# Sharing the expert sum of a PEER layer between VectorE and GpSimd, row by row

## The reference

```python
q = jnp.einsum('td,de->te', xb, wq).reshape(PEER_BLOCK, PEER_HEADS, 2, PEER_DH)
s = jnp.einsum('thpc,hpnc->thpn', q, subkeys).astype(jnp.float32)
...
g = jax.nn.softmax(top, axis=-1)
hid = jnp.einsum('thkd,td->thk', u_tab[idx], xb).astype(jnp.float32)
act = (g * jax.nn.gelu(hid)).astype(xb.dtype)
return jnp.einsum('thk,thkd->td', act, v_tab[idx])
```

## Time and profile before

| | |
|---|---|
| median of 3 runs | 4849.47 us (4844.11 to 4852.52) |
| the profiled execution | 4842.91 us, its span 4841.2 us |
| busy: PE / DVE / ACT / POOL | 68% / 65% / 21% / 28% of the span |
| DVE adds L1805 | 640, 817.9 us, 1278 ns each |
| DVE dots L1789 | 640, 779.9 us, 1219 ns each |
| POOL gathers L1600 | 640, 776.8 us, 1214 ns each; 2112.2 us idle before them |
| DMA moved | 1579.68 MB, mean 326 GB/s |
| peer rows of tiles 0 to 4 | from about 640 us to 3680 us; the tail is what follows |

### The profile page before, as it was taken

How to read it: one execution, slowest core, us unless ns; L and a number is a source line. 1 busy time by engine, 2 the same in 40 slices (tenths; PEclk the granted TensorE clock), 3 DMA queues, 4 the chain that set the end, 5 groups by cost and what they waited for, 6 DMA issues and landing times. The chain is left out here.

```text
span 4841.2 us, 38032 instructions
## 1 busy us (share of the span) xinstructions
PE 3289.7 (68%) x10576; PEld 1748.2 (36%) x10576; DVE 3157.7 (65%) x6031; ACT 993.4 (21%) x2018; POOL 1372.4 (28%) x1287
## 2 busy tenths in 40 slices
PE   8679786455987687446455556985904777777776
PEld 6466542333544333334211112432401333333322
DVE  0121277896767688889766665887687666766754
ACT  1120111243211110235323231221101111111121
POOL 0000023322223234312111112332234454444432
PEclk9789898566998899567666667997957998989989
DMA  5343489777989899866799998998879999999988
GB/s 212 103 138 144 161 326 372 284 251 283 360 329 374 313 369 399 295 221 223 287 412 408 407 399 307 378 360 326 351 247 372 421 421 421 421 421 421 421 359 335
DMA packets 311757, 1579.68 MB, mean 326 GB/s; under 512 B 36536, under 2 KB 96108, under 8 KB 155823
## 3 DMA queue, kind: packets, MB, share of 16 engines
q0 software_dynamic: 158288, 1151.42, 60.1%
q1 hardware_dynamic: 122750, 377.41, 20.5%
q10 hardware_dynamic: 30560, 49.03, 2.7%
HBM read 1526.49 MB, written 50.99 MB: 326 GB/s over the span
## 5 line engine op out<-in xcount | busy, mean ns | idle before, releaser
L1600 POOL DMA_INDIRECT peer_row<-in_peer_uv,peer_staged x640 | 776.8, 1214 | 2112.2 <-DVE peer_y L1805 2013.4
L1789 DVE SCALAR_TENSOR_TENSOR peer_row<-peer_row,peer_x 128x1024 f32<-128x1024 f32 x640 | 779.9, 1219 | 183.4 <-DMA peer_row<-in_peer_uv,peer_staged 151.3
L1805 DVE SCALAR_TENSOR_TENSOR peer_y<-peer_row,peer_coef,peer_y 128x1024 f32<-128x1024 f32 x640 | 817.9, 1278 | 0.0
L1968 PE MATMUL tail_y<-peer_row,tail_diag 128*128 128x512 f32 x896 | 441.2, 650 | 308.5 <-ACT tail_diag L1981 308.5
L1968 PE MATMUL tail_y<-tail_row,tail_diag 128*128 128x512 f32 x896 | 432.8, 641 | 130.9 <-ACT tail_diag L1981 130.9
L245 PE MATMUL pr_b<-pr_xT,pr_w 128*128 128x256 f32 (+2 forms) x1152 | 389.8, 502 | 110.0 <-DMA pr_xT<-in_xT 79.2
L829 PE MATMUL gs_gp<-gs_xT,gs_w 128*128 128x256 f32 (+2 forms) x1152 | 393.5, 496 | 51.1 <-DMA gs_w<-in_w_gate 46.2
L1968 PEld LDWEIGHTS tail_y<-peer_row,tail_diag 128*128 128x128 f32 x896 | 181.7, 208 | 567.2 <-issue 384.8
L1927 POOL DMA_INDIRECT peer_row<-in_peer_uv,tail_staged x224 | 259.3, 1158 | 307.1 <-PE tail_y L1968 237.0
L1927 POOL DMA_INDIRECT tail_row<-in_peer_uv,tail_staged x224 | 253.3, 1131 | 281.0 <-PE tail_y L1968 245.0
L245 PEld LDWEIGHTS pr_b<-pr_xT,pr_w 128*128 128x128 f32 x1152 | 225.6, 197 | 272.7 <-issue 180.3
(11 more groups left out here) (216 smaller groups left out, 4350.9 us busy)
## 6 DMA issues: line engine op xcount, KB each, us to landing
sa_kc<-in_cache_k SPq DMA_DIRECT2D x128, 512.0 KB, 14.4
sa_vc<-in_cache_v SPq DMA_DIRECT2D x128, 512.0 KB, 12.9
pr_w<-in_w_in SPq DMA_DIRECT2D x27, 2048.0 KB, 10.9
gs_w<-in_w_gate SPq DMA_DIRECT2D x36, 1024.0 KB, 9.6
rt_w<-in_w_q SPq DMA_DIRECT2D x24, 1024.0 KB, 8.8
gs_w<-in_w_br SPq DMA_DIRECT2D x24, 512.0 KB, 5.0
gs_w<-in_w_br SPq DMA_DIRECT2D x12, 1024.0 KB, 7.8
mx_w<-in_w_out SPq DMA_DIRECT2D x6, 2048.0 KB, 12.3
```

The source lines that it names most:

```text
L1600: pool.indirect_dma_start(out=self.row[b][:], out_offset=None, in_=dr["peer_uv"], in_offset=bass.IndirectOffsetOnAxis(ap=self.staged[slot] ...
L1789: v.scalar_tensor_tensor(out=self.row[b][:, 0:D], in0=self.row[b][:, 0:D], scalar=1.0, in1=self.x1[:], op0=ALU.mult, op1=ALU.mult, accum_o ...
L1805: v.scalar_tensor_tensor(out=self.y[:], in0=self.row[b][:, D:2 * D], scalar=self.coef[:, col:col + 1], in1=self.y[:], op0=ALU.mult, op1=AL ...
L1968: done = pe.matmul(part[:], diag[r % (2 * ROWS)][:], row[place(j, k)][:, D + hf * 512:D + (hf + 1) * 512], start=j == 0 and k == 0, stop=j ...
```

## The change

In the front's tiles the rows with odd k (1 and 3 of each unit, 320 of 640) are no longer added by DVE. POOL does it, directly before the gather that reuses the buffer: a tensor_scalar scales the v half in place by its coefficient, a tensor_tensor adds it to a second accumulator. This is the tile `out`, which is free between the store of one tile and the norm of the next; the first such row of a tile writes it with the tensor_scalar alone. The norm first adds `out` to `y` on DVE. POOL's loops are unrolled in Python, since each wait now has a constant value. In the first gathers of the tail POOL also adds the two odd rows of tile 4's last unit.

```diff
         def fetch(pool, m, k, slot):
 
             b = slot % 2 * ROWS + k
-            pool.wait_ge(self.added, ROWS * m + ROWS + k + 1)
-            apart(pool, dr["unwaited"])
+            if m >= 2 and k % 2:
+                self.add_second(pool, m - 2, k)
+                pool.wait_ge(self.added_second, self.second_through(m - 2, k))
+            elif m >= 2:
+                pool.wait_ge(self.added, self.first_through(m - 2, k))
             pool.indirect_dma_start(
...
+    def add_second(self, pool, m, k):
+
+        n, j = divmod(m, UNITS)
+        b, col = j % 2 * ROWS + k, ROWS * j + k
+        v_row, coef = self.row[b][:, D:2 * D], self.coef[:, col:col + 1]
+        pool.wait_ge(self.weighted, m + 2)
+        if j == 0 and k == 1:
+            if n:
+                pool.wait_ge(self.y_stored, 16 * n)
+            pool.tensor_scalar(self.out[:], v_row, coef, None, ALU.mult).then_inc(self.added_second, 1)
+        else:
+            pool.tensor_scalar(v_row, v_row, coef, None, ALU.mult).then_inc(self.scaled_second, 1)
+            pool.wait_ge(self.scaled_second, self.second_through(m, k) - n - 1)
+            pool.wait_ge(self.added_second, self.second_through(m, k) - 1)
+            pool.tensor_tensor(self.out[:], self.out[:], v_row, op=ALU.add).then_inc(self.added_second, 1)
...
     def norm(self, v, n):
-        v.wait_ge(self.added, ROWS * UNITS * n + ROWS * (self.units_of(n) + 3))
-        if n >= self.tail:
+        if n < self.tail:
+            v.wait_ge(self.added, self.first_through(UNITS * n + UNITS - 1, ROWS - 2))
+            v.wait_ge(self.added_second, self.second_through(UNITS * n + UNITS - 1, ROWS - 1))
+            v.tensor_tensor(self.y[:], self.y[:], self.out[:], op=ALU.add).then_inc(self.joined, 1)
+            v.wait_ge(self.joined, n + 1)
...
-        if adding:
+        if adding and k % 2 == 0:
             self.add(v, pn, pj, k)
...
-                        pool.wait_ge(self.added, added_through(r - len(self.row)))
-                        apart(pool, dr["unwaited"])
+                        m, k = divmod(r - len(self.row), ROWS)
+                        if k % 2:
+                            self.add_second(pool, m, k)
+                            pool.wait_ge(self.added_second, self.second_through(m, k))
+                        else:
+                            pool.wait_ge(self.added, self.first_through(m, k))
...
-                if n == first and j == 0:
+                if n == first and j == 0 and k % 2 == 0:
                     self.add(v, n - 1, UNITS - 1, k)
```

More of the change, by code:

```diff
@@ L1561, in __init__ @@
         self.added = sem("added")
+        self.added_second = sem("added_second")
+        self.scaled_second = sem("scaled_second")
+        self.joined = sem("joined")
         self.gelued = sem("gelued")
@@ L1603, in fetch, with tile @@
             ).then_inc(self.row_loaded[b], 16)
-        def units(pool, n, i):
-            for s in range(self.BLOCK):
-                m = n * UNITS + i * self.BLOCK + s
-                pool.tensor_copy(self.staged[s][:], self.index[:, bass.ds((i * self.BLOCK + s) * ROWS, ROWS)])\
+        def tile(pool, n):
+            pool.wait_ge(self.picked, self.KSTEP * n + self.KSTEP)
+            pool.tensor_copy(self.index[:], self.index_next[:]).then_inc(self.indexed, 1)
+            pool.wait_ge(self.indexed, n + 1)
+            for j in range(UNITS):
+                if j == (LATE if n in self.late else 0):
+                    load_score(pool, n + 1)
+                m = n * UNITS + j
+                slot = j % self.BLOCK
+                pool.tensor_copy(self.staged[slot][:], self.index[:, ROWS * j:ROWS * (j + 1)])\
                     .then_inc(self.staging, 1)
@@ L1614, in units @@
                 for k in range(ROWS):
-                    fetch(pool, m, k, s)
-        def tile(pool, n, late=False):
-            blocks, half = UNITS // self.BLOCK, LATE // self.BLOCK
-            pool.wait_ge(self.picked, self.KSTEP * n + self.KSTEP)
-            apart(pool, dr["unwaited"])
-            pool.tensor_copy(self.index[:], self.index_next[:]).then_inc(self.indexed, 1)
-            pool.wait_ge(self.indexed, n + 1)
-            apart(pool, dr["unwaited"])
-            if not late:
-                load_score(pool, n + 1)
-            start = 0
-            if late:
-                with pool.Fori(start, half) as i:
-                    units(pool, n, i)
-                load_score(pool, n + 1)
-                start = half
-            with pool.Fori(start, blocks) as i:
-                units(pool, n, i)
+                    fetch(pool, m, k, slot)
         @block.gpsimd
@@ L1639, in _, with first_through, late_through, second_through @@
             load_score(pool, 0)
-            n = 0
-            for stop in sorted({0, *self.late}):
-                if stop - n > 1:
-                    with pool.Fori(n, stop) as i:
-                        tile(pool, i)
-                elif stop - n == 1:
-                    tile(pool, n)
-                tile(pool, stop, late=stop in self.late)
-                n = stop + 1
-            assert n == self.tail
+            for n in range(self.tail):
+                tile(pool, n)
+    def first_through(self, m, k):
+        return 3 * ROWS + m * (ROWS // 2) + k // 2 + 1
+    def late_through(self, r):
+        before = ROWS * UNITS * self.tail
+        return 3 * ROWS + before // 2 + r - before + 1
+    def second_through(self, m, k):
+        return m * (ROWS // 2) + k // 2 + 1
+    def add_second(self, pool, m, k):
[12 more added lines that the diff above has]
+            pool.tensor_tensor(self.out[:], self.out[:], v_row, op=ALU.add).then_inc(self.added_second, 1)
     def scalar_open(self, act, part):
@@ L1802, in add @@
             v.wait_ge(self.weighted, UNITS * n + j + 2)
-        v.wait_ge(self.added, ROWS * UNITS * n + ROWS * (j + 3) + k)
+        v.wait_ge(self.added, self.first_through(UNITS * n + j, k) - 1)
         col = ROWS * j + k
@@ L1905, in nth @@
             return per_tile * n + ROWS * j + k
-        def added_through(r):
-            return 3 * ROWS + r + 1
+        added_through = self.late_through
         @block.gpsimd
@@ L1979, in diagonals @@
                     r = nth(n, j, k)
-                    act.wait_ge(self.added, added_through(r - 2 * ROWS))
+                    if r - 2 * ROWS >= nth(first, 0, 0):
+                        act.wait_ge(self.added, added_through(r - 2 * ROWS))
                     act.activation(diag[r % (2 * ROWS)][:], ident[:], ACT.Copy,
```

3 lines of the change are left out of this document (2 added, 1 removed).

## The result

| | before | after |
|---|---|---|
| median of 4 runs each (same chip) | 4846.8 us | 5352.2 us |
| lowest to highest | 4842.4 to 4852.5 | 5344.1 to 5357.7 |
| ratio, 95% interval | | 1.104 (1.102 to 1.106) |
| profiled run, its span | 4842.9, 4841.2 us | 5344.1, 5342.3 us |

The change makes the kernel 10.4% slower. The forecast was 5220 us, 7.6%, in a range of 4980 to 5460.

The account below looks back on a forecast made before the run. Row transfers bound dense projections (DVE next), DVE the prompt stage, cache transfers the sample stage. Projections +125, middle stages +170, prompt and sample +43, tile ends +30, tail below 5: about +370 on 4842.9, forecast 5220 us, range 4980 to 5460.

Parts of the forecast that it names:

- POOL's price for a row, 2.9 us: On POOL, from its copies' slope: tensor_scalar about 1.0 us plus tensor_tensor about 1.9 us; upper bound 5.8 us a row.
- The third rival: POOL's arithmetic much slower than its copy, toward 5.8 us a row: unit 23.3 us, total 5700 us; chance 7%.
- The unit without collisions, 12.7 us: POOL's four-row unit unhindered: copy 0.19, three gaps of 0.89, gathers 3.76, 0.31 between gathers, row work 5.8 us.
- Unrolling: 0: Unrolling POOL's loops changes nothing, since the register instructions cost less than the gathers they stand between.
- Collisions, +4.8 us a unit: POOL held by DVE: four new instructions 0.8 us each, gathers 1.1, copy 0.24, late even-row adds 0.3; unit 17.5 us.
- DVE held, two thirds of POOL's work: POOL's reads hold DVE's dots and adds 3.9 us a unit, less 2.56 us of adds removed: +1.3 us net.
- Dense projections, +125 us: Projection stages, 32 units: from 13.6 us to POOL's 17.5 us, +3.9 us each.
- The middle stages, +170 us: All other stages of about 17 us, 85 units: +2.0 us each, between +0.5 and +3.9.
- Prompt and sample, +43 us: Prompt and sample stages, 43 units of 25.2 us: POOL has time, DVE's holding costs +1 us each.
- Ends of tiles, +30 us: Five tile ends: a DVE join of about 1.2 us and POOL's wait for the store of `out`, 6 us each.
- Tail, below 5 us: Tail from 3680 us: only two of four rows of one unit are touched, below 5 us.
- The first rival's gain, -144 us: The offload works, POOL neither holding DVE nor hardly held; unit about 13.9 us, total 4705 us; chance 6%.

Follow-up runs that it names:

- the writing kernels: The changed kernel with memsets to an unread tile instead of POOL's arithmetic, odd rows dropped: 5.2 us a row 5027.21 us, 2.4 us a row 4799.25 us.
- the kernels above: The changed kernel, 5352 us; it without POOL's arithmetic, odd rows and join, 4760 us; the latter with POOL memsets of 5.2 us a row, 5027 us.
- The long write: Changed kernel with eight memsets to an unread tile, 5.2 us a row, replacing POOL's scaling and adding; odd rows and join dropped: 5027.21 us, ratio 1.038.

## Why the prediction was right, and where its sizes were off

The sign and the mechanism were right: POOL's unit becomes the bound, and its reads hold DVE. The time, 5352 us, is 132 us above the forecast and inside its range. That it is no further off owes something to luck, since misses of opposite sign met. By the forecast's own steps:

- **POOL's price for a row, 2.9 us.** Mis-sized: 2.84 + 2.34 = 5.2 us. The tensor_scalar, taken at 1.0, is the larger miss; the copies' slope gave the copy and not the arithmetic. The third rival, arithmetic slower than a copy, was true at 90% of its 5.8 us. Its unit, 23.3 us, and its time, 5700 us, were not: it kept the forecast's gaps and collisions, which were both too large, and the dense unit is 19.1.
- **The unit without collisions, 12.7 us.** With the measured prices it is 0.19 + 0.27 + 3.76 + 0.30 + 2 x 0.27 + 2 x (2.86 + 2.34 + 0.08) = 15.6 us. The price's miss (+4.6) was partly met by the three gaps of 0.89 that are 0.27 in unrolled code (-1.9), which I had read as a wait and priced as one. "Unrolling: 0" was right in time (ratio 1.000).
- **Collisions, +4.8 us a unit.** 19.1 - 15.6 = 3.5 in the dense stretches: somewhat less. A POOL instruction is held by 0.08 us (tensor_scalar, 2937 against 2860) or 0.28 (tensor_tensor, 2619 against 2340) on average, much less than the 0.8 taken: 0.7 us a unit instead of 3.2. The gathers, at 1415 ns against 940 alone, give 1.9 instead of 1.1, the copy 0.3; POOL's waits for a late add would be the rest.
- **DVE held, two thirds of POOL's work.** Right in direction, and shown by the writing kernels; right in size too. Without the adds DVE is busy 2793.6 us, with POOL's reading 3330.4: 537 us more, of which 6 are the join, or 3.3 us a unit where 3.9 was taken. Net of the relief, DVE's busy time rose by 172.7 us, about +1.0 us a unit where +1.3 was taken. 326 of the 537 us are the dots and adds. 80 sit in the small instructions that make the coefficients: over 128x4 elements 272 of them took 451 ns on average, 156 before. Most of the rest is in the front's own instructions, as the scans into `at_sums` (93.0 us before, 130.6 now).
- **Dense projections, +125 us:** +134, by two misses that cancel. The dense unit lost 19.1 - 13.6 = 5.5 us and not 3.9. But only 22 of the 32 units had stood in the dense stretches; 22 x 5.5 = 121 us, and the ten others, around the stages' starts and gates, lost little.
- **The middle stages, +170 us:** +321, the term that failed. "On average already near 17.5" let me take half of the dense units' loss. With POOL's ideal unit at 15.6 and its real one at 19.1, these 85 units had no slack: with the 30 us of the tile ends taken out, 291 us, they lost 3.4 us each, near the upper end I had named (+3.9). By the stage table of the kernels above, the relief gave these stages 37 us, POOL's time took 163 and the reading, with the ends of tiles, 195.
- **Prompt and sample, +43 us:** +33. The slack was there: with 25 us a unit, POOL at 70% and 57% busy had room, and the long write cost these stages 2.8 us. The 33 are 67 us of reading less 37 us of relief.
- **Ends of tiles, +30 us:** the join waited 28.4 us in all for POOL's last addition and took 1.22 us itself; the wait of POOL for the store of `out`, which I had feared, was 0.6 us. About the right sum, by the other half of the term.

```profile
L1824 DVE TENSOR_TENSOR peer_y<-peer_y,peer_out 128x1024 f32<-128x1024 f32 x5 | 6.1, 1221 | 28.4 <-POOL peer_out L1662 28.4
```

- **Tail, below 5 us:** +10.9. The long write has +7.0 there, without reading; what makes it is open.
- **The first rival's gain, -144 us,** was more than the idea holds: adds that cost nothing give 82 us. The middle stages gave 37 us and not 128, the prompt and sample stages 37 and not 56. What else limits the middle stages' units was not separated.
- **The range.** Its terms give 5020 and 5430 us; the prediction's "about 5010" and "about 5440" are 10 us wider.

What stays open: whether the reading's 325 us are DVE's holding or POOL's, since one changes the other; why a scaling and an addition together cost more than the sum of both; and how the cost would grow with POOL's share between a quarter and a half.

## What to carry to other kernels

An idle engine isn't a free one: price what it is to do by its own instruction (a copy says nothing of a tensor_scalar), and ask what it shares with the engine that is to be relieved. Where the relieved engine works on two SBUF inputs, an elementwise reader on GpSimd can take back all that it gives and more, as here (by the pages, 364 us of DVE's busy time given and 537 taken); a kernel that drops the moved work shows first how much there is to win, here 1.7%, and one that only writes for as long shows what the reading costs.

## What was not expected of the hardware

- On POOL over 128x1024 float32: memset 0.95 us, copy 1.03, tensor_scalar 2.84 (2.78 with an immediate), tensor_tensor add 2.34, tensor_tensor multiply with the second input broadcast from one column 1.89. Scaling by a tensor_scalar is slower than by a tensor_tensor, though in the kernel the shorter one gained nothing.
- The tensor_scalar holds DVE only in its first microsecond or so. A second instance beside those above, where the dot starts 0.19 us into it and ends 2.21 us into it, 1.0 us and then its own 1.21:

```profile
2006.60 2.86 POOL L1657 TENSOR_SCALAR peer_out<-peer_row,peer_coef 128x1024 f32<-128x1024 f32 x1
2006.79 2.02 DVE L1801 SCALAR_TENSOR_TENSOR peer_row<-peer_row,peer_x 128x1024 f32<-128x1024 f32 x1
```

- A DVE instruction of 128x4 elements, 0.16 us alone, takes 1.94 us behind POOL's addition (730.83 us): reading little doesn't spare an instruction from being held.
